# Two-block transformer forward on one core: a new order of TensorE's steps and of its PSUM banks in the forgetting attention

## The chip, the cores and the metric

One NeuronCore of a Trainium2 chip runs one program. The metric is device time in microseconds from launch to end. The kernel before takes 2098.56 us, the median of 3 runs that lie between 2098.52 and 2100.52 us.

## The reference, cut to what matters

The reference applies two transformer blocks to x, 512 tokens of width 1024. The change touches only the mixer of the first block (and the place where it meets the second step of that block, the memory attention):

```python
z = h @ w_in                        # h = rms_norm(x); columns: a, g, q, k, v, f
u = a * sigmoid(g)
u = causal_depthwise_conv(u, conv_w, conv_b)         # 31 taps, 512 channels
u = silu(layer_norm(u, conv_ln_g, conv_ln_b))
log_f = log_sigmoid(f_logit + b_forget)
# forgetting attention, 8 heads of 64, blocks of 128 queries, causal
logits = q k^T * scale + cum[q] - cum[k]             # cum = cumsum(log_f)
att = softmax(mask(logits)) @ v
y = concat([u, att]) @ w_out
...
mem_n = rms_norm(mem)                                # 256 memory tokens
k_mem = mem_n @ w_mk                                 # used one stage later
```

## The kernel before, in words

Tokens lie along the free dimension (512 columns), features along the partitions. Each engine has one hand-written program in `build`, and semaphores tie them together; every instruction starts in the order of its own program. All products are float32 split in a high and a low part, so that one product is three matmuls (`mm3`, three calls of line 159). Weights come in chunks of 1 MB (`CHUNKS`): SP loads chunk n into one of two staging tiles, ACT copies the high part (`weights(n)`), POOL subtracts it to get the low part (`weights(n)` of POOL, tile WL), and TensorE waits for both before a chunk's first product. ACT's copy of chunk n waits until TensorE is done with chunk n-2.

PSUM has eight banks. `open_bank` takes the next in turn and waits until its last tenant is freed; two banks are reserved (`co`) as sums of the convolution for as long as VectorE works on it.

The stage of the forgetting attention runs so on TensorE: eight steps of gemm `ag`, then the values (`v`, four banks, 96 matmuls over chunks 6 and 7), a small column sum `ms`, then the query and key tiles. A tile `qk n` (24 matmuls of 512 columns) holds queries (n even) or keys (n odd) of two heads. Tiles 0, 1 and 2 come first, then the logits of head 0, `fox_s(0)` (four mask products and eight products), then tile 3, and then a loop over the eight heads h:

- `fox_t(h)`: ten transposes of the normalised weights PP into three banks `ft`.
- `fox_s(h+1)`: the next head's logits, in three banks `fs`.
- `qk_tile(h+4)`, for h up to 3: a whole tile.
- `fox_pv(h)`: 12 matmuls with V, in bank `fo`.
- for h = 0 the spread of the memory norm `mr`; for h = 4 the total `cmu` of the convolution's channels; for h = 5 the memory keys of chunk 12 (`mem_k(0, 0, 1)`); for h = 6 one column sum `cq2`, one tile of chunk 13 and the spread `crs`; for h = 7 the other tile of chunk 13.

Then gemm `wo` (w_out) starts with chunk 14 and walks k = 0 to 7; k = 0 to 3 is the convolution's output (HH, HL), k = 4 to 7 are the heads in pairs (CATH, CATL).

What the other engines do for a head: VectorE takes the four row maxima (`fox_max`, TENSOR_REDUCE), ACT the exponentials, VectorE the reciprocals (`fox_rcp`), ACT the four norms into PP (`fox_norm`). After the transposes ACT writes PTH (`fox_turned`) and VectorE PTL, which also frees the `ft` banks. After `fox_pv` ACT writes CATH (`fox_high`) and VectorE CATL (`fox_low`), which frees `fo`. For a tile `qk n` VectorE scales it in place (`qk_out`), ACT copies the high parts (`qk_high`), VectorE subtracts the low ones, which frees the bank, and POOL makes twins of the high parts for the other half of the partitions (`twins`).

Beside that runs the depthwise convolution with its 31 taps for each of four groups of channels: VectorE does most (`convolve(n, 3)` issues the next n taps of a list), ACT and POOL share 25 taps of group 1: ACT makes a product into one of four tiles TP (`products`), POOL adds it (`taps`); product w waits for tap w-4. POOL sums the groups (`cacc`), TensorE's `cmu` turns that into a mean, VectorE subtracts it (`xc`), ACT squares (`csq`), POOL adds the squares (`c2acc`), the column sum `cq2` and a root give the norm, and after `crs` VectorE scales the groups (`xn_`), ACT applies the silu and VectorE writes HL. The memory tokens are scaled on VectorE (`scaled_memory`), split by ACT (`memory_high`) and POOL.

## Time and profile before

| what | value |
|---|---|
| median of 3 runs | 2098.56 us |
| the profiled execution's own time | 2100.5 us |
| its span, first to last instruction | 2098.7 us |
| PE busy | 2011.9 us, 96% |
| DVE / ACT / POOL busy | 1272.0 / 861.7 / 983.0 us |
| mean granted clock of TensorE | 0.990 |

Matmuls are pipelined: a matmul's duration in a row is longer than the distance to the next one, and the distance is what a stream costs. An idle time stands in square brackets behind a row with what ended it. A row may merge several instructions (x10) and then hide waits between them.

### The profile page before, as it was taken

The numbers are of one execution on the slowest core, as the hardware profiler recorded it, in microseconds if no ns is written. First come the engines' busy times: TensorE is split into PE (matmuls) and PEld (weight loads), VectorE is DVE, ScalarE is ACT, GpSimd is POOL, SyncE is SP. The second block draws the span as 40 slices with busy tenths as digits, with TensorE's granted clock in tenths as the row PEclk, the third lists the DMA queues.
The fourth block names the chain that finished last, engine by engine and source line by source line (L and its number), as shares of the span: only waits on it lengthen the run. The fifth ranks groups of instructions, "written<-read, shape, count | busy, mean of one in ns | idle before, by whom it ended". The sixth has DMA issues, their size and how long they took to land.

```text
span 2098.7 us, 23678 instructions
## 1 busy us (share of the span) xinstructions
PE 2011.9 (96%) x9667; PEld 1672.6 (80%) x9667; DVE 1272.0 (61%) x1568; ACT 861.7 (41%) x1254; POOL 983.0 (47%) x476
## 2 busy tenths in 40 slices
PE   6999989999999999999999999999998999999997
PEld 4777778778888887787888888878887888888886
DVE  7677845462245435663677775545679657778644
ACT  5746775631122234774443333232322244333322
POOL 5579454454444433123444444444667654444443
PEclk9999999999999999999999999999999999999999
DMA  6432123112222230121222222215222312222221
GB/s 206 154 123 81 41 81 106 65 71 101 101 99 86 97 113 27 43 71 47 71 86 98 101 101 100 84 63 185 101 71 101 121 61 101 100 101 92 89 101 40
DMA packets 35041, 193.00 MB, mean 92 GB/s; under 512 B 4400, under 2 KB 4992, under 8 KB 15413
## 3 DMA queue, kind: packets, MB, share of 16 engines
q1 hardware_dynamic: 34932, 191.49, 26.1%
q8 instruction: 76, 1.25, 0.3%
q14 instruction: 33, 0.26, 0.0%
HBM read 177.77 MB, written 13.64 MB: 91 GB/s over the span
## 4 chain that ended last, share of the span: by engine, by line
PE 77%; DVE 11%; ACT 6%; POOL 4%; issue 2%; DMA 0%; SPq 0%; ACTq 0%; DVEq 0%; POOLq 0%
PE ps L159 73%; PE ps L158 3%; DVE TMP L182 2%; POOL WL L182 1%; POOL CO L182 1%; DVE X L182 1%; DVE X L194 1%; DVE YL L182 1%; PE ps L167 1%; DVE ps L194 1%; POOL YF L182 1%; DVE ps L182 1%; ACT WH L175 1%; ACT PP L176 0%; DVE VG L182 0%
## 5 line engine op out<-in xcount | busy, mean ns | idle before, releaser
L182 POOL TENSOR_TENSOR WL<-W,WH 128x2048 fp32r<-128x2048 f32 (+3 forms) x165 | 650.5, 3948 | 860.5 <-ACT WH L175 857.0
L159 PE MATMUL ps<-HH,WL 128*128 128x512 f32 (+1 forms) x1408 | 545.6, 388 | 15.4 <-DVE HL L194 7.9
L159 PE MATMUL ps<-HH,WH 128*128 128x512 f32 (+1 forms) x1408 | 538.8, 383 | 0.0
L159 PE MATMUL ps<-HL,WH 128*128 128x512 f32 (+1 forms) x1408 | 538.8, 383 | 0.0
L175 ACT ACTIVATE WH<-W 128x2048 fp32r<-128x2048 f32 (+2 forms) x145 | 269.4, 1858 | 316.8 <-PE ps L159 316.8
L159 PEld LDWEIGHTS ps<-HH,WL 128*128 128x128 f32 x1408 | 265.3, 188 | 74.9 <-DVE HL L194 9.9
L159 PEld LDWEIGHTS ps<-HH,WH 128*128 128x128 f32 x1408 | 265.2, 188 | 51.9
L159 PEld LDWEIGHTS ps<-HL,WH 128*128 128x128 f32 x1408 | 265.6, 189 | 50.7 <-issue 0.2
L182 DVE TENSOR_TENSOR MRL<-MID,MRH 128x512 fp32r<-128x512 f32 x76 | 177.4, 2365 | 162.3 <-ACT MRH L175 162.3
L159 PE MATMUL ps<-MRH,WL 128*128 128x512 f32 x608 | 238.2, 392 | 3.3 <-ACT PAD L175 2.2
L159 PE MATMUL ps<-MRH,WH 128*128 128x512 f32 x608 | 236.7, 389 | 0.0
L159 PE MATMUL ps<-MRL,WH 128*128 128x512 f32 x608 | 236.6, 389 | 0.0
L182 DVE TENSOR_TENSOR MID<-TMP,TMP 128x512 f32<-128x512 f32 x44 | 175.8, 3996 | 30.7 <-ACT TMP L176 30.7
L175 ACT ACTIVATE PAD<-ps 128x512 f32<-128x512 f32 x88 | 52.6, 600 | 273.0 <-PE ps L159 273.0
L194 DVE SCALAR_TENSOR_TENSOR TMP<-PAD,PAR,TMP 128x512 f32<-128x512 f32 x176 | 140.7, 800 | 6.2
L159 PEld LDWEIGHTS ps<-MRH,WL 128*128 128x128 f32 x608 | 114.2, 188 | 28.3 <-ACT PAD L175 3.0
L159 PEld LDWEIGHTS ps<-MRL,WH 128*128 128x128 f32 x608 | 114.2, 188 | 23.9 <-issue 0.5
L159 PEld LDWEIGHTS ps<-MRH,WH 128*128 128x128 f32 x608 | 114.1, 188 | 23.9
L182 DVE TENSOR_TENSOR TMP<-ps,TMP 128x512 f32<-128x512 f32 x36 | 24.8, 690 | 111.4 <-PE ps L159 104.8
L182 POOL TENSOR_TENSOR TMP<-TMP,TMP 128x512 f32<-128x512 f32 x47 | 62.7, 1334 | 63.2 <-ACT TMP L176 61.5
L194 DVE SCALAR_TENSOR_TENSOR X<-X,ps 128x512 f32<-128x512 f32 (+1 forms) x36 | 22.5, 627 | 110.4 <-PE ps L159 110.3
L188 DVE TENSOR_SCALAR TMP<-PAD,PAR 128x512 f32<-128x512 f32 x88 | 42.2, 480 | 72.4 <-ACT PAD L175 72.4
(370 smaller groups left out, 3284.3 us busy)
## 6 DMA issues: line engine op xcount, KB each, us to landing
W<-in_up SPq DMA_DIRECT2D x44, 1024.0 KB, 4.8
W<-in_down SPq DMA_DIRECT2D x22, 1024.0 KB, 4.8
W<-in_w_up SPq DMA_DIRECT2D x16, 1024.0 KB, 4.8
W<-in_w_down SPq DMA_DIRECT2D x16, 1024.0 KB, 4.8
W<-in_hy_in SPq DMA_DIRECT2D x12, 1024.0 KB, 4.8
kd<-STG SPq DMA_DIRECT2D x36, 256.0 KB, 2.0
KB<-kd SPq DMA_DIRECT2D x8, 1024.0 KB, 5.8
W<-in_win_ag SPq DMA_DIRECT2D x4, 1024.0 KB, 4.8
```

What stands on the lines that cost most here:

```text
L158: return self.eng.matmul(out, lhs, rhs, start=start, stop=stop, skip_group_check=True)
L159: return self.eng.matmul(out, lhs, rhs, start=start, stop=stop)
L167: return QUIET if self.eng is None else self.eng.transpose(out, src, ident)
L175: return self.eng.activation(out, src, fn, scale=scale)
L182: return QUIET if self.eng is None else self.eng.tensor_tensor(out, a, b, op)
L188: return self.eng.tensor_scalar(out, a, s1, None, o1)
L194: return self.eng.scalar_tensor_tensor(out=out, in0=a, scalar=s, in1=b, op0=o1, op1=o2)
```

## The change

TensorE: tiles `qk` 0 and 1 move ahead of the values, and w_in's first query and key chunk moves ahead of the values' chunks (it becomes chunk 6, the values' 7 and 8). After the values come `ms`, the logits of head 0 and tile 2. In the loop, tiles 3 to 7 come one a head for h = 0 to 4, each cut in halves of 12 matmuls before and after the next head's logits; for h = 5 the memory keys of chunk 12 take their place, cut in the same way. The fourth mask product of a head moves behind the products of the first three blocks. `cmu` moves from h = 4 to h = 2. Banks are no longer taken in turn but named (`on(i)`): `here` are the three banks of this head's logits, `there` the others, and they change places at each head's end. For h = 6 the column sum runs over the four tiles of squares instead of one sum of them, and `crs` moves to h = 7. The first chunk of w_out is written out as `out_first`, in the order k = 4, 5, 6, 0, 1, 2, 3, 7, in banks `there[0:2]`.

VectorE: the taps are spread anew (2, 6 and 20 before the values' low parts, 3 after each of three of them, 6 in head 0, 3 and all that are left in head 1); `xc`, the memory's scaling and the last scaling move to other heads. ACT: `weights`, `products`, `qk_high` and the memory's parts stand elsewhere; the squares of the convolution go to POOL. POOL: two more taps ahead of `weights(8)`, and the memory's low parts ahead of the last twins. SP's program is unchanged, but the order of its loads follows `CHUNKS`.

```diff
@@ -53,8 +53,8 @@
 CHUNKS = [
-    ("dft_cs", 0, 2048), ("dft_kx", 0, 256), *[("win_ag", i, 2048) for i in range(4)], *[("win_v", i, 2048) for i in range(2)],
-    *[("win_qk", i, 2048) for i in range(4)], *[("w_mk", i, 2048) for i in range(2)],
+    ("dft_cs", 0, 2048), ("dft_kx", 0, 256), *[("win_ag", i, 2048) for i in range(4)], ("win_qk", 0, 2048),
+    *[("win_v", i, 2048) for i in range(2)], *[("win_qk", i, 2048) for i in range(1, 4)], *[("w_mk", i, 2048) for i in range(2)],
     *[("w_out", i, 2048) for i in range(4)],
     *[("w_mv", i, 2048) for i in range(2)],
     *[("w_mq", i, 2048) for i in range(2)], *[("w_mo", i, 2048) for i in range(2)],
...
@@ -745,6 +745,21 @@
     gemm("ag", CH["win_ag"][2:4], 8, 2, feat, lambda k: ("hn", 0, k), base=4, head=False)
+    def on(i):
+        turn[0] = i
+    def qk_steps(n, first, last):
+        wh, wl = chunk(CH["win_qk"][n // 2])
+        ps = bank("qk", n) if first else open_bank("qk", n)
+        for k in range(first, last + 1):
+            col = (2 * k + n % 2) * 128
+            ins = pe.mm3(ps[:], wh[:, col:col + 128], wl[:, col:col + 128], *feat(k), k == 0, k == 7)
+        if last == 7:
+            ins.then_inc(*up(acc, ("qk", n), *[("w_used", CH["win_qk"][n // 2])] * (n % 2)))
+    qk_steps(0, 0, 7)
+    qk_steps(1, 0, 7)
...
+    g0, g1 = bank_of["qk", 0], bank_of["qk", 1]
+    v0, v1, v2, v3 = [bank_of["v", b] for b in range(4)]
+    c0, c1 = bank_of["co", 0], bank_of["co", 1]
+    on(v0)
     column_sum([(("ms",), MSQ[:, 0, :], ("msum", 1), None, ("ms",))], nb=2)
-    def qk_tile(n):
-        if n >= 8:
-            return
-        wh, wl = chunk(CH["win_qk"][n // 2])
-        ps = open_bank("qk", n)
-        for k in range(8):
-            col = (2 * k + n % 2) * 128
-            ins = pe.mm3(ps[:], wh[:, col:col + 128], wl[:, col:col + 128], *feat(k), k == 0, k == 7)
-        ins.then_inc(*up(acc, ("qk", n), *[("w_used", CH["win_qk"][n // 2])] * (n % 2)))
-        for i in (0, 2, 3):
-            open_bank("fs", h, max(i, 1))
-        for i in range(4):
+        def mask(i):
+            if i != 1:
+                on(places[max(i - 1, 0)])
+                open_bank("fs", h, max(i, 1))
             nk = 128 * (i + 1)
             pe.mm(logits(h, i)[:, nk - 128:nk], IDR[:], MKR[:], i != 1, False, True)
+        for i in range(3):
+            mask(i)
...
         for i in range(4):
+            if i == 3:
+                mask(3)
...
-    qk_tile(0)
-    qk_tile(1)
-    qk_tile(2)
-    fox_s(0)
-    qk_tile(3)
+    def cat_tile(k):
+        return feat(k) if k < 4 else (CATH[k - 4][:], CATL[k - 4][:])
+    def out_first(places):
+        n = CH["w_out"][0]
+        wh, wl = chunk(n)
+        for m, i in enumerate(places):
+            on(i)
+            open_bank("wo", m, hold=True)
+        for k in (4, 5, 6, 0, 1, 2, 3, 7):
+            pe.wait_ge(*at("cat", k))
+            for m in range(2):
+                col = (2 * k + m) * 128
+                rh, rl = cat_tile(k)
+                ins = pe.mm3(bank("wo", m)[:], wh[:, col:col + 128], wl[:, col:col + 128], rh, rl, k == 4,
+                             k == 7)
+                if k == 7:
+                    ins.then_inc(*up(acc, ("wo", m), *[("w_used", n)] * m))
+                    close("wo", m)
+    fox_s(0, (g0, g1, v1))
+    on(v2)
+    qk_steps(2, 0, 7)
+    here, there = [g0, g1, v1], [v0, v2, v3]
     for h in range(8):
-        fox_t(h)
+        fox_t(h, here)
+        if h < 5:
+            on(there[2])
+            qk_steps(h + 3, 0, 3)
+        if h == 5:
+            mem_k(0, (0, 1), 0, 3, (c0, c1))
         if h < 7:
-            fox_s(h + 1)
+            fox_s(h + 1, (there[0], there[1], here[0]))
+        if h < 5:
+            qk_steps(h + 3, 4, 7)
+        if h == 5:
+            mem_k(0, (0, 1), 4, 7)
+        if h == 6:
+            on(there[2])
+            column_sum([(("cq2",), CO2[:, j, :], ("csq", j), None, ("cq2",) if j == 3 else None)
+                        for j in range(4)])
+            mem_k(1, (0,), 0, 7, (here[2],))
         if h == 7:
-            mem_k(1, 1)
-        qk_tile(h + 4)
-        fox_pv(h)
+            mem_k(1, (1,), 0, 7, (c0,))
+            on(c1)
+            spread("crs", slot=20)
+        fox_pv(h, here[1])
         if h == 0:
+            on(here[2])
             spread("mr", slot=28, nb=2)
-        if h == 4:
-            total("cmu", ap=DG[:], need=("cacc", 3))
+        if h == 2:
             close("co", 0)
             close("co", 1)
-        if h == 5:
-            mem_k(0, 0, 1)
-        if h == 6:
-            column_sum([(("cq2",), CO2[:, 0, :], ("c2acc", 3), None, ("cq2",))])
-            mem_k(1, 0)
-            spread("crs", slot=20)
-    def cat_tile(k):
-        return feat(k) if k < 4 else (CATH[k - 4][:], CATL[k - 4][:])
+            on(c0)
+            total("cmu", ap=DG[:], need=("cacc", 3))
+        here, there = [there[0], there[1], here[0]], [there[2], here[1], here[2]]
...
@@ -864,7 +911,8 @@
-    gemm("wo", CH["w_out"], 8, 2, cat_tile, lambda k: ("cat", k))
+    out_first(there[0:2])
+    gemm("wo", CH["w_out"][1:], 8, 2, cat_tile, lambda k: ("cat", k), base=2, head=False)
...
@@ -1472,24 +1520,11 @@
     act.act(MSQ[:], MX0[:], ACT.Square, ROOT_D).then_inc(*out(("msq",)))
-    weights(7)
-    products(5, 8)
-    weights(8)
-    for b in range(4):
-        act.wait_ge(*at("v", b))
-        act.wait_ge(*at("inv", "xs"))
-        act.act(VH[:, b, :], bank("v", b)[:], ACT.Identity, SM[:, 4 + b:5 + b]).then_inc(*out(("vv", b, "hi")))
-        if b == 3:
-            weights(9)
-        products(9 + 2 * b, 10 + 2 * b)
-    root(("ms",), 24, "eps6", 2)
     def qk_high(n):
-        if n >= 8:
...
@@ -1498,6 +1533,22 @@
+    weights(7)
+    products(5, 8)
+    qk_high(0)
+    products(9, 12)
+    qk_high(1)
+    weights(8)
+    products(13, 16)
+    weights(9)
+    for b in range(4):
+        act.wait_ge(*at("v", b))
+        act.wait_ge(*at("inv", "xs"))
+        act.act(VH[:, b, :], bank("v", b)[:], ACT.Identity, SM[:, 4 + b:5 + b]).then_inc(*out(("vv", b, "hi")))
+        if b < 3:
+            products(17 + b, 17 + b)
+    root(("ms",), 24, "eps6", 2)
     def expo(group, dst, nk, scale, slot, *need):
...
@@ -1561,40 +1612,43 @@
         act.wait_ge(*now(act_tile))
         high(HH[:, j, :], CO[:, j, :], ("cat", j))
-    qk_high(0)
-    products(17, 20)
-    qk_high(1)
-    products(21, 24)
-    qk_high(2)
+    weights(10)
     fox_exp(0)
     fox_norm(0)
-    qk_high(3)
+    products(20, 22)
+    qk_high(2)
     for h in range(8):
-        if h > 5:
-            mem_k_high(*((0, 1), (2,))[h - 6])
         fox_turned(h)
+        if h == 0:
+            products(23, 24)
+        if h == 6:
+            mem_k_high(0, 1)
         if h < 7:
             fox_exp(h + 1)
             fox_norm(h + 1)
-        if h == 4:
-            memory_high(0, 3)
-        if h == 7:
+        else:
+            weights(14)
+            mem_k_high(2)
             for j in range(4):
                 silu(j)
-        qk_high(h + 4)
+        if h == 1:
+            weights(11)
+        if h == 3:
+            memory_high(0, 3)
+        if h == 4:
+            memory_high(4, 7)
+        if h == 5:
+            weights(13)
+        if h == 6:
+            root(("cq2",), 16, "eps6", 4, 1.0 / 512)
+        if h < 5:
+            qk_high(h + 3)
         fox_high(h)
         if h == 0:
             act.wait_ge(*at("mr"))
             act.copy(MRS[:], bank("mr")[:, 0:256]).then_inc(*out(("mrs",), ("free", "mr")))
-        if h == 5:
-            memory_high(4, 7)
-            for j in range(4):
-                act.wait_ge(*at("xc", j))
-                act.act(CO2[:, j, :], CO[:, j, :], ACT.Square, 512.0 ** -0.5).then_inc(*out(("csq", j)))
-            weights(13)
-        if h == 6:
-            root(("cq2",), 16, "eps6")
-            weights(14)
+        if h == 2:
+            weights(12)
     mem_k_high(3)
...
@@ -2226,30 +2280,29 @@
     gated(3)
-    for b in range(4):
-        convolve(4, 3)
-    for b in range(4):
-        dve.wait_ge(*at("vv", b, "hi"))
-        dve.stt(VL[:, b, :], bank("v", b)[:], SM[:, 4 + b:5 + b], VH[:, b, :].bitcast(F), ALU.mult,
-                ALU.subtract).then_inc(*out(("vv", b), ("free", "v", b)))
-        convolve(2, 3)
...
                 *[("free", "qk", n)] * e)
-        if n < 2:
-            convolve(4, 3)
+    convolve(2, 3)
+    qk_out(0)
+    convolve(6, 3)
+    qk_out(1)
+    convolve(20, 3)
+    for b in range(4):
+        dve.wait_ge(*at("vv", b, "hi"))
+        dve.stt(VL[:, b, :], bank("v", b)[:], SM[:, 4 + b:5 + b], VH[:, b, :].bitcast(F), ALU.mult,
+                ALU.subtract).then_inc(*out(("vv", b), ("free", "v", b)))
+        convolve((3, 3, 3, 0)[b], 3)
...
@@ -2293,45 +2346,48 @@
-    qk_out(0)
-    qk_out(1)
-    qk_out(2)
+    def centred(first, last):
+        for j in range(first, last + 1):
+            dve.wait_ge(*at("cmu"))
+            dve.stt(CO[:, j, :], bank("cmu")[:], -1.0 / 512, CO[:, j, :], ALU.mult, ALU.add).then_inc(
+                *out(("xc", j), *[("free", "cmu")] * (j == 3)))
     fox_max(0)
     fox_rcp(0)
-    qk_out(3)
+    qk_out(2)
     for h in range(8):
-        if h > 5:
-            mem_k_low(*((0, 1), (2,))[h - 6])
         for j in range(3):
             q = turned(j)
             low(PTL[:, q], bank("ft", h, j)[:, 0:q.stop - q.start], PTH[:, q], ("pt", h, j), ("free", "ft", h, j))
+        if h == 6:
+            mem_k_low(0, 1)
         if h < 7:
             fox_max(h + 1)
-            convolve(3, 3)
-            if h in (4, 5):
-                scaled_memory(4 * h - 16, 4 * h - 15)
+            if h == 1:
+                convolve(3, 3)
+            if h in (3, 4):
+                scaled_memory(4 * h - 12, 4 * h - 9)
             fox_rcp(h + 1)
-            if h in (4, 5):
-                scaled_memory(4 * h - 14, 4 * h - 13)
-        convolve(4, 3)
+        if h == 0:
+            convolve(6, 3)
+        if h == 1:
+            convolve(200, 3)
+        if h in (3, 4):
+            centred(2 * h - 6, 2 * h - 5)
         if h == 7:
-            for j in range(4):
-                low(HL[:, j, :], CO[:, j, :], HH[:, j, :], ("cat", j))
-        qk_out(h + 4)
-        fox_low(h)
-        if h == 4:
-            convolve(200, 3)
-            dve.wait_ge(*at("cmu"))
-            for j in range(4):
-                dve.stt(CO[:, j, :], bank("cmu")[:], -1.0 / 512, CO[:, j, :], ALU.mult, ALU.add).then_inc(
-                    *out(("xc", j), *[("free", "cmu")] * (j == 3)))
-        if h == 6:
-            inverse(("cq2",), 16, [("col", "crs")])
             weights(CH["w_out"][0])
             dve.wait_ge(*at("crs"))
             for j in range(4):
                 dve.tt(CO[:, j, :], CO[:, j, :], bank("crs")[:], ALU.mult).then_inc(
                     *out(("xn_", j), *[("free", "crs")] * (j == 3)))
+            mem_k_low(2)
+            for j in range(4):
+                low(HL[:, j, :], CO[:, j, :], HH[:, j, :], ("cat", j))
+        if h < 5:
+            qk_out(h + 3)
+        fox_low(h)
+        if h == 6:
+            inverse(("cq2",), 16, [("col", "crs")])
     mem_k_low(3)
     def post(s, Y, g, g2):
...
@@ -3037,12 +3093,13 @@
     weights(7)
-    taps(5, 8)
+    taps(5, 10)
     weights(8)
-    taps(9, 14)
+    taps(11, 16)
     weights(9)
-    taps(15, 24)
+    taps(17, 19)
...
@@ -3050,20 +3107,28 @@
     next_rows(6)
-    twins(5)
-    next_rows(7)
-    twins(6)
-    weights(12)
-    twins(7)
     for j in range(1, 4):
         pool.wait_ge(*at("tap", j, 30))
         if j > 1:
             pool.wait_ge(*at("cacc", j - 1))
         pool.tt(DG[:], CO[:, 0, :] if j == 1 else DG[:], CO[:, j, :], ALU.add).then_inc(*out(("cacc", j)))
-    for k in range(8):
-        pool.wait_ge(*at("hm", k, "hi"))
-        pool.low(HML[:, k, :], tmp("mn", k)[:, 0:256], HMH[k]).then_inc(*out(("hm", k), ("tf", "mn", k)))
-    add_up(CO2[:, 0, :], lambda j: CO2[:, j, :], 3, ("csq",), ("c2acc",))
+    next_rows(7)
+    twins(5)
+    weights(12)
+    def memory_low(first, last):
+        for k in range(first, last + 1):
+            pool.wait_ge(*at("hm", k, "hi"))
+            pool.low(HML[:, k, :], tmp("mn", k)[:, 0:256], HMH[k]).then_inc(*out(("hm", k), ("tf", "mn", k)))
+    memory_low(0, 3)
+    twins(6)
+    memory_low(4, 7)
+    twins(7)
+    for j in range(4):
+        pool.wait_ge(*at("xc", j))
+        pool.wait_ge(*at("qk", 7))
+        pool.tt(CO2[:, j, :], CO[:, j, :], CO[:, j, :], ALU.mult).then_inc(*out(("csq", j)))
     weights(13)
```

## Rows read from the trace of the kernel before

**Rows 1.** The page: the span, and busy time of each engine.

```profile
span 2098.7 us, 23678 instructions
PE 2011.9 (96%) x9667; PEld 1672.6 (80%) x9667; DVE 1272.0 (61%) x1568; ACT 861.7 (41%) x1254; POOL 983.0 (47%) x476
```

**Rows 2.** Stretches: length, busy time of PE, PEld, DVE, ACT, POOL, PEclk, DMA share, GB/s.

```profile
152.00:306.00 154.00, 139.64 (x732) 118.46 (x731) 107.21 (x191) 110.66 (x216) 98.05 (x76) 0.96 0.19 69
205.00:211.00 6.00, 5.86 (x18) 5.16 (x19) 5.14 (x11) 2.90 (x10) 3.97 (x7) 0.50 0.43 167
265.00:270.00 5.00, 4.70 (x22) 4.60 (x23) 4.41 (x12) 3.11 (x11) 0.00 (x0) 0.66 0.00 0
1408.00:1410.00 2.00, 2.00 (x9) 1.66 (x10) 2.00 (x4) 2.00 (x4) 0.60 (x1) 1.00 0.00 0
```

**Rows 3.** Who PE waited for, 150 to 300 us: total, times, longest.

```profile
PE ps L158 <- DVE PTL L182: 3.8, 2, 2.8
...
PE ps L158 <- DVE CATL L182: 3.2, 4, 1.3
```

**Rows 4.** Timeline of PE: start, duration, line, operation, idle before.

```profile
152.13 0.47 PE L159 MATMUL ps<-WH,HL 128*128 128x512 f32 x1
...
173.98 0.58 PE L158 MATMUL ps<-ONE,MSQ 128*128 128x96 f32 x4
...
201.79 3.18 PE L167 MATMUL ps<-IDT,PP 128*128 128x128 f32 x10 [3.32 <-DVE ps L194]
...
249.53 0.39 PE L158 MATMUL ps<-PTH,VL 128*128 128x512 f32 x1
...
251.39 1.28 PE L167 MATMUL ps<-IDT,PP 128*128 128x128 f32 x10
253.37 0.63 PE L158 MATMUL ps<-MKR,IDR 128*128 128x128 f32 x4 [0.70 <-DVE CATL L182]
...
255.16 0.40 PE L158 MATMUL ps<-PTH,VL 128*128 128x512 f32 x1
...
280.82 1.08 PE L158 MATMUL ps<-ONE,CO 128*128 128x96 f32 x8
...
1407.91 0.50 PE L159 MATMUL ps<-HH,WL 128*128 128x512 f32 x1 [2.44 <-POOL HL L182]
```

**Rows 5.** Timeline of POOL: taps of group 1, and the low part of a chunk.

```profile
162.34 5.41 POOL L182 TENSOR_TENSOR CO<-CO,TP 128x512 f32<-128x512 f32 x4
167.70 4.63 POOL L182 TENSOR_TENSOR WL<-W,WH 128x2048 fp32r<-128x2048 f32 x1
```

**Rows 6.** Timeline of ACT.

```profile
218.08 0.37 ACT L175 ACTIVATE MRS<-ps 128x256 f32<-128x256 f32 x1
...
286.48 1.90 ACT L175 ACTIVATE WH<-W 128x2048 fp32r<-128x2048 f32 x1
...
288.54 1.36 ACT L175 ACTIVATE PTH<-ps 128x512 fp32r<-128x512 f32 x3
289.92 1.28 ACT L176 ACT_TABLE_LOAD   x1
291.21 0.82 ACT L176 ACTIVATE CO<-CO,PAR 128x512 f32<-128x512 f32 x1
...
296.83 0.59 ACT L175 ACTIVATE CATH<-ps 64x512 fp32r<-64x512 f32 x1
```

**Rows 7.** Timeline of DVE.

```profile
222.17 2.06 DVE L194 SCALAR_TENSOR_TENSOR ps<-U,PAR,ps 128x512 f32<-128x512 f32 x3
...
226.97 0.69 DVE L194 SCALAR_TENSOR_TENSOR ps<-ps,TMP 128x512 f32<-128x512 f32 x1
228.32 1.41 DVE L182 TENSOR_TENSOR QKB<-ps,QKA 64x512 fp32r<-64x512 f32 x2 [0.66 <-ACT QKA L175]
...
254.79 1.67 DVE L206 TENSOR_REDUCE SM<-ps 128x1 f32<-128x128 f32 x4
...
257.61 0.18 DVE L200 RECIPROCAL SM<-SM 128x4 f32<-128x4 f32 x1 [0.24 <-ACT PP L173]
```

33 lines of the change are left out of this document (17 added, 16 removed).

## The prediction

> **What bounds the kernel now.** I read the page first: PE is busy for 2011.9 of 2098.7 us [rows 1], so only what TensorE does, and where it waits, sets the end. Second, the stretches: in the 154.0 us of this stage PE is busy for 139.6, so it stands still for 14.4 us, and its granted clock is 0.96 there [rows 2]. Third, who PE waited for: two low parts of VectorE hold 7.0 us of it, PTL with one wait of 2.8, and CATL, which frees the bank of the head before, with four [rows 3]. Fourth, the timeline, for what the busy time hides. Ten transposes take 3.18 us at 201.79 and 1.28 at 251.39 [rows 4]: 1.9 us are waits inside a merged row. And the clock: after the wait of 3.32 us it is at 0.50 (1.2 GHz in place of 2.4) from 205 to 211, which loses 3.0 us, and after the wait of 2.8 us it averages 0.66 for 5 us, which loses 1.7 [rows 2, 3, 4]. Together the stage holds 14.4 + 1.9 + 3.0 + 1.7 = 21.0 us in which PE does not work at its speed. This is the most that the change could take away; outside the stage it touches nothing.
>
> **What PE does a head.** 96 matmuls of 512 columns take 173.98 - 152.13 = 21.85 us, 0.228 each: a tile of 24 takes 5.4, its half 2.7 [rows 4]. The product with V takes 251.39 - 249.53 = 1.9, the logits 255.16 - 253.37 = 1.8, the transposes some 1.0 (1.28 less the tail that overlaps the next) [rows 4]. From the end of the logits to the reciprocals pass 257.61 - 255.16 = 2.45 us, to the end of the maxima 1.3 [rows 4, 7].
>
> **What the change wins.** The first transposes no longer follow a wait for tile 3, the halves put 2.7 us between the transposes and the next logits, so CATL (3.2 us of waits) is covered, and a tile covers head 5's chain, which was bare. I count all 21.0 us as gone, and then count what comes in their place, edit by edit.
>
> **Work, +3.0.** One column sum becomes four. One is 8 matmuls in 1.08 us [rows 4]; three more are 3.2, a little less as rows overlap: 3.0. ACT's squares and POOL's sums become four products on POOL, 5.41 / 4 = 1.35 each by its adds [rows 5], in head 5; between 0.6 and 1.4 each they end ahead of the column sum of head 6. Nothing on the path.
>
> **A: the second chunk of the values, +3.7.** PE starts tile 0 at 152.13 as it started the values, ends tile 1 10.9 us later at 163.0 and the values' first half at 173.9; there it needs chunk 8. ACT copies chunk 8 only behind products(9, 12) and qk_high(1). POOL's taps begin at 162.34 as before, 1.35 each [rows 5]. Product 12 waits for tap 8, at 162.34 + 4 x 1.35 = 167.7, and ends some 0.7 later (0.82 for an activation of the same size [rows 6]): 168.4. The two high copies and two twins behind it take 2.5 (0.59 for one of 64x512 [rows 6]), the copy 1.90: 172.8. POOL has then ended its six taps (170.4), takes 4.63 for the low part [rows 5] and is done at 177.4. PE waits from 173.9 to 177.6. Before, the eighth chunk's low part stood two taps earlier on POOL and had no tile's copies ahead of it on ACT. SP's loads keep their order by chunk and 1 MB each; each is free to go more than 10 us ahead of its copy, so none of them counts.
>
> **The first transposes, +0.8.** The values end at 188.4, logits and tile 2 at 196.1. On ACT stand behind the values: a copy 0.6, the root with its table 1.5, chunk 10 1.9, the table of the exponential 1.3, four exponentials 2.2 (of the 2.45 above); reciprocals and norms follow, the first at 196.4, the last ending at 198.3. So the transposes end 1.6 later than PE could. Bounds 0 and 1.6; I take the middle.
>
> **B: tile 4, +3.3.** By the head's times PE ends the transposes of head 0 at 198.7, half of tile 3 at 201.4, logits at 203.2, the other half at 205.9, V at 207.8, mr at 208.3 and the transposes of head 1 at 209.3. Tile 4 goes to the bank there[2], which is here[2] of head 0: the place of mr. It is free when ACT has copied MRS, behind qk_high(3) and CATH. VectorE has reciprocals at 205.7 and then six taps of 0.66 (2.06 for three, overlapping [rows 7]) before it scales tile 3: 209.7, scaled 210.4; ACT's two copies 1.2, CATH 0.6, MRS 0.37 [rows 6]: 212.5. PE waits 3.3.
>
> **C: head 3's logits, +5.5.** From 212.6 PE does half a tile, logits (217.2), half a tile, V, transposes, half a tile: 225.5. The mask of head 3 goes to tile 4's bank. VectorE ends the maxima at 218.5, has 3 and then 11 taps left in head 1 (14 x 0.66 = 9.2: 227.7), and scaling and low parts of tile 4 take 2.8 (226.97 to 229.73 [rows 7]): 230.5. The second mask wants the bank of head 1's V, whose low part CATL comes 0.7 later. 5.0 and 0.5. Before, the same taps stood seven to a head, each group behind other cover.
>
> **Small waits, +1.2.** In head 5 the halves are 1.5 us each, so the norms end behind them; in head 6 CATH of head 5 stands behind chunk 13's copy (1.90 [rows 6]), and a bank waits for it; head 6's logits want the twins of tile 7, behind four low parts on POOL. My bounds are 0 and 2.5; I take the middle.
>
> **D: the first product of w_out, +6.0.** This is what I find most telling. After head 7's swap there[1] is here[1] of head 7, the bank of its V. out_first opens both banks before its first matmul, so PE waits until VectorE has written CATL of head 7. That is the last step of all: from the end of the transposes, T, ACT does PTH 1.36, chunk 14 1.90, one memory key 0.3, then table, four silus and CATH, 289.92 to 297.42 = 7.5 [rows 6], then VectorE 0.7: T + 11.8. PE needs 2.9 for the memory tile, 1.0 for the spread and 1.9 for V: T + 5.8. Before, the eight steps began with this chain still running, since nothing but k = 7 needs it; the order 4, 5, 6, 0 to 3, 7 would still allow it, the bank doesn't.
>
> **The clock, +6.8.** A, B, C and D are each as long as the 3.32 and 2.8 us that let the clock fall, or longer. The rows bound what one such wait costs behind it: nothing after 2.44 us at 1407.91 (clock 1.00), 1.7 us at 265, 3.0 us at 205 [rows 2, 4]. I take 1.7 for each of four, the middle one.
>
> **Sum.** 3.0 + 3.7 + 0.8 + 3.3 + 5.5 + 1.2 + 6.0 + 6.8 = 30.3, less 21.0: +9.3 us. It is made against the profiled execution, whose span is 2098.7 and whose own time is 2100.5, 1.9 above the median; I add it to the median: 2098.6 + 9.3 = **2107.9 us**. About 0.2%, 4.2 us, is what a measurement of this kernel can tell from no change.
>
> **Where a page speaks against the change.** A table load on ACT takes 1.28 us here, and the next instruction starts at once, 289.92 to 291.21 [rows 6]. The Trainium skill, page "ScalarE: Activation LUTs", section "What ACT_TABLE_LOAD costs", adds a drain of some 1.38 us to each switch, 2.66 in all. The chain of the first transposes holds two switches and that of D one; by the page those waits would grow by 3 x 1.38, an estimate of 4.1 us. The trace disagrees with it.
>
> **The rivals.**
> 1. VectorE keeps ahead of the heads (not slower). 37 of the taps are done by the end of the values. If tile 3 is scaled before PE ends tile 3's second half and V, which means by 207.8 where I have 210.4, B and C vanish with their two falls of the clock: 9.3 - 3.3 - 5.5 - 3.4 = -2.9, 2095.7 us. It decides at the six taps in head 0. For it: 46.8 us of the stage VectorE is idle now [rows 2]. Against it: those taps are written ahead of the scaling. Chance 0.12, of which 0.08 for under 2094.4, as small terms fall away too.
> 2. The clock holds as after 2.44 us [rows 2, 4]: 9.3 - 6.8 = +2.5, 2101.1 us. Chance 0.08: all four waits are longer than the two that let it fall.
> 3. All at the upper bounds: clock 3.0 each, 1.6 and 2.5 for the small ones: 25.6 + 12.0 - 21.0 = +16.6, 2115.2 us. Chance 0.09.
> 4. A switch of tables costs the chains of the first transposes and of D a second load's time, three times 1.28 [rows 6]: 9.3 + 3.8 = +13.1, 2111.7 us. Chance 0.03, since no load of the trace does it. The drain of the Trainium skill's page named above would be such a mechanism.
> My forecast keeps 0.68, of which 0.04 lies under 2102.8 us. Slower: 0.64 + 0.09 + 0.03 = 0.76; the same: 0.04 + 0.08 + 0.04 = 0.16; faster 0.08. The range, 2099 to 2115, leaves out rival 1 and the edge of rival 3.
>
> **What would show it.** In the profile after: WL of a chunk named as what ended a PE wait near 174 to 178; a wait of 3 to 4 us ended by ACT MRS near 210; one near 226 to 231 ended by VectorE's QKA or QKB low part; a wait of about 6 us right ahead of w_out's first matmul, ended by CATL; PEclk 0.5 behind several of them; CATL no longer behind four waits of the middle heads. Wrong if the stage is shorter than 154 us, if VectorE's taps end before head 1's logits, or if w_out starts with no wait.

## The result and the profile after

The changed kernel takes 2106.5 us (median of seven runs, 2104.8 to 2107.2) where the kernel before takes 2099.9: a ratio of 1.0033, 95% interval 1.0023 to 1.0043. A second measurement, beside three of the experiments below and on their chip, gave 2106.9 (six runs, 2104.0 to 2113.1) against 2098.7, 1.0043 (1.0031 to 1.0055). So the change costs 7 to 8 us. The forecast was 2107.9, slower, with a range of 2099 to 2115.

The top of the page, to set beside [rows 1]:

```profile
span 2103.0 us, 23723 instructions
PE 2009.2 (96%) x9691; PEld 1672.3 (80%) x9691; DVE 1272.3 (61%) x1568; ACT 860.4 (41%) x1250; POOL 983.5 (47%) x477
```

PE is busy for 2.7 us less than before in a span 4.3 us longer. What the stage lost stands in two views. First, who PE waited for from 150 to 320 us (total, times, longest), beside [rows 3]:

```profile
PE ps L159 <- DVE CATL L182: 6.1, 1, 6.1
PE ps L158 <- DVE QKA L182: 4.2, 1, 4.2
PE ps L159 <- POOL WL L182: 3.7, 1, 3.7
PE ps L159 <- ACT MRS L175: 3.3, 1, 3.3
PE ps L158 <- DVE CATL L182: 1.6, 2, 1.3
```

The rows of before are gone: no PTL, and CATL only twice between heads. Four waits that before did not have take their place, and each is the longest of its row. Second, the stretches behind three of those waits (A, C and D below), beside [rows 2]; the column ahead of the last two is the clock that was granted:

```profile
152.00:306.00 154.00, 132.87 (x716) 114.38 (x715) 106.91 (x191) 106.57 (x210) 95.43 (x76) 0.94 0.19 68
...
176.00:178.00 2.00, 1.79 (x4) 1.50 (x5) 2.00 (x4) 0.67 (x1) 1.92 (x3) 0.50 0.45 90
...
234.00:236.00 2.00, 2.00 (x8) 1.85 (x8) 1.96 (x6) 0.47 (x3) 1.84 (x3) 0.50 0.88 369
...
300.00:302.00 2.00, 1.99 (x5) 1.62 (x6) 0.32 (x1) 1.99 (x3) 0.00 (x0) 0.50 0.00 0
302.00:304.00 2.00, 2.00 (x7) 1.52 (x6) 0.00 (x0) 0.75 (x1) 1.17 (x1) 0.50 0.00 0
304.00:306.00 2.00, 2.00 (x7) 1.60 (x6) 0.00 (x0) 0.00 (x0) 2.00 (x1) 0.66 0.00 0
306.00:308.00 2.00, 2.00 (x10) 1.65 (x9) 0.00 (x0) 0.00 (x0) 1.41 (x1) 1.00 0.00 0
```

In the same 154 us PE is busy for 132.9 us where it was for 139.6 [rows 2], at a clock of 0.94 for 0.96. Behind each wait stand some 3.4 us at 1.2 GHz, behind the last twice as much.

PE's own rows date the four waits A to D and show the four column sums:

```profile
176.21 0.77 PE L159 MATMUL ps<-WH,HL 128*128 128x512 f32 x1 [3.68 <-POOL WL L182]
...
213.57 0.77 PE L159 MATMUL ps<-HH,WL 128*128 128x512 f32 x1 [3.35 <-ACT MRS L175]
...
232.64 0.44 PE L158 MATMUL ps<-MKR,IDR 128*128 128x128 f32 x2 [4.20 <-DVE QKA L182]
...
278.71 3.71 PE L158 MATMUL ps<-ONE,CO 128*128 128x96 f32 x32
282.20 0.36 PE L159 MATMUL ps<-HM,WL 128*128 128x256 f32 x1
...
300.01 0.77 PE L159 MATMUL ps<-CATH,WL 128*128 128x512 f32 x1 [6.07 <-DVE CATL L182]
```

To compare traces I use one measure: the **stage** runs from the start of the first tile and the values (10.9 us ahead of the values' first matmul in the changed kernel, that matmul itself before) to the start of the matmul behind w_out's first 48, so that a wait between the two counts to the stage; the **rest** is all behind it. Before: 152.13 to 305.98, 153.8 us. After: 150.6 to 313.5, 162.9 us, or 9.1 us more.

### The profile page after: what moved, and what is told of

Same layout as the page of the kernel before. It is cut to its first block, busy times and chain, and to the rows that moved or that the text cites. A ratio compares the mean times of both kernels' runs of the same rounds, so it can differ in the third digit from the quotient of the medians.

```text
span 2103.0 us, 23723 instructions
## 1 busy us (share of the span) xinstructions
PE 2009.2 (96%) x9691; PEld 1672.3 (80%) x9691; DVE 1272.3 (61%) x1568; ACT 860.4 (41%) x1250; POOL 983.5 (47%) x477
## 3 DMA queue, kind: packets, MB, share of 16 engines
q8 instruction: 76, 1.25, 0.3%
## 4 chain that ended last, share of the span: by engine, by line
PE 78%; DVE 11%; ACT 6%; POOL 4%; issue 2%; DMA 0%; SPq 0%; ACTq 0%; DVEq 0%; POOLq 0%
PE ps L159 73%; PE ps L158 3%; DVE TMP L182 2%; POOL WL L182 1%; DVE X L182 1%; DVE X L194 1%; DVE YL L182 1%; DVE ps L194 1%; PE ps L167 1%; POOL CO L182 1%; POOL YF L182 1%; DVE ps L182 1%; ACT WH L175 1%; DVE VG L182 0%; ACT PM L173 0%
## 5 line engine op out<-in xcount | busy, mean ns | idle before, releaser
L159 PE MATMUL ps<-MRL,WH 128*128 128x512 f32 x608 | 236.6, 389 | 0.0
```

Source lines behind the costliest of these rows:

```text
L159: return self.eng.matmul(out, lhs, rhs, start=start, stop=stop)
```

## The experiments

All are edits of the changed kernel, except where said. The rows of the tables are worked out from PE's timelines and from stretches. The first table gives for each trace the start of its stage, the stage, the rest, how often the clock fell in the rest ahead of the last matmul (each time some 3.4 us at 1.2 GHz, from stretches of 2 us), and the median of the runs beside it.

Start, stage and rest add up to the span of the one execution that was traced, which can lie at either end of its runs: 2104.8 us was the lowest of seven in the first trace of the changed kernel. The kernel before has 2098.5 to 2098.7 us beside these medians, and 2099.9 beside the first of the changed kernel. Where A was not edited, its wait is 3.6 to 3.7 us in five traces and 2.2 to 2.3 in five others (see the end), so stages are compared with the trace of the changed kernel that has the same A: the second for "free banks", "work in the wait", "free banks and chunk 15" and "whole tiles", the first for the others.

| trace | starts | stage | rest | falls | median |
|---|---|---|---|---|---|
| before | 152.1 | 153.8 | 1792.8 | 3 | 2098.6 |
| changed | 150.6 | 162.9 | 1789.5 | 1 | 2106.5 |
| changed, again | 151.8 | 161.0 | 1793.5 | 4 | 2106.9 |
| free banks | 155.1 | 154.5 | 1795.6 | 4 | 2106.5 |
| free banks, again | 152.3 | 157.1 | 1795.8 | 4 | 2106.5 |
| chunk 8 first | 152.0 | 159.0 | 1789.5 | 1 | 2102.3 |
| MRS first | 152.2 | 159.7 | 1789.4 | 1 | 2107.6 |
| taps moved | 152.2 | 160.4 | 1792.6 | 3 | 2106.1 |
| work in the wait | 152.1 | 158.2 | 1792.7 | 3 | 2107.2 |
| free banks and chunk 15 | 153.6 | 153.8 | 1793.9 | 4 | 2103.1 |
| one sum | 152.4 | 160.8 | 1791.2 | 2 | 2108.5 |
| whole tiles | 155.0 | 168.8 | 1792.6 | 3 | 2117.3 |
| all four | 150.6 | 145.8 | 1789.4 | 1 | 2092.0 |
| all five | 152.0 | 143.8 | 1790.8 | 1 | 2088.6 |

**D: free banks for w_out's first products.**

```diff
-            out_first(there[0:2])
+            out_first((there[2], here[2]))
```

> Edit: w_out's first two products take the banks of head 7's first tile half and its last (free long before) in place of the pair in which head 7's V lies; nothing else. My theory: the wait of 6.07 us ended by CATL of head 7, right ahead of w_out, is one for the bank alone, and the half clock in the 6 us behind it (a loss of 2.7 us by the stretches) comes from it. Both go: at most a wait of 0.4 us for the low part of chunk 14 is left, and the time falls by 8.3 us against the changed kernel, to about 2098.2 us. Rival: PE would wait for the data of head 7 all the same, since the eight steps reach k = 7 too early; then the wait only moves behind the seventh step and the gain is under 3 us. A third: the clock falls later anyway, gain 6.

Measured: 2106.5 us, ratio to before 1.0034 (1.0022 to 1.0046). The whole time did not move, where 8.3 us less were expected; the stage did, by 6.5 us and by 5.8 in a second trace. PE's rows at the place where the 6.07 stood, and 48 matmuls later:

```profile
296.49 0.47 PE L159 MATMUL ps<-CATH,WL 128*128 128x512 f32 x1 [0.54 <-issue]
...
309.58 0.47 PE L159 MATMUL ps<-HH,WL 128*128 128x512 f32 x1 [1.96 <-POOL WL L182]
```

```profile
312.00:314.00 2.00, 2.00 (x6) 1.62 (x5) 0.00 (x0) 0.00 (x0) 2.00 (x1) 0.50 0.83 344
```

The wait of 6.07 is 0.54, so it was for a bank and not for data: k = 7 comes 9.6 us later and finds CATL written. The low part of chunk 15 is next to be late, 1.96 us, and the clock falls behind that wait (0.50 from 312 to 314). That the rest took the gain back is followed up in the last experiment.

**D and what came behind it.** On ACT `weights(15)` goes behind `mem_k_high(2)` of head 7, ahead of the silus, with the free banks as above.

> Edit: the free banks for w_out's first two products, as before, and on ACT the high copy of chunk 15 goes ahead of the table load and the four silus; with the banks alone w_out's second chunk then waited 1.96 us for the low part that POOL makes of that copy. My theory: both waits go, and at most 0.6 us ahead of the first product is left; w_out's first chunk takes 10.9 us, at full clock. Stage: 153.5 to 154.5 us, that is 8.9 less than the changed kernel's; whole time 2097 to 2099 if the falls of the clock elsewhere are as many as in the changed kernel. Rival: the copy delays the silus by 1.9 us and the fifth to eighth step of w_out wait for them: then 2 us are lost again between the third step and the last.

Measured: 2103.1 us, 1.0022 (1.0014 to 1.0031). The stage is 153.8 us, 7.2 under the changed kernel's second trace, which shares with it the short wait at A. The second wait is gone; 0.75 us for the low part of the first silu took its place, ended by DVE HL, a small piece of the rival. The stage came as expected, the whole time is 4 us over its 2097 to 2099: the rest has four falls here.

**The clock at D alone.** Work of no use in the wait:

```diff
+            pe.wait_ge(*at("free", "ft", 7, 0))
+            keep_busy(24, CH["w_out"][0], "ft", 7, 0)
             out_first(there[0:2])
```

> Edit: 24 matmuls of no use run in the changed kernel's wait ahead of w_out's first product, into a bank of head 7 that is free; some 5.5 us of work in a wait of 6.07. Nothing else. My theory: the wait keeps its end, but the granted clock stays at 1.00 in the 8 us behind it, which loses 3.4 us in the changed kernel; w_out's first chunk takes 10.9 to 11.2 us in place of 13.5 to 14.4, the time falls by 3.4, to about 2103. Rival: the clock falls behind these 8 us for what went before (two transposes, a spread, products) and the dummies change nothing: same time.

PE's rows and the stretches behind them:

```profile
293.00 5.66 PE L158 MATMUL ps<-WH,IDR 128*128 128x512 f32 x24
299.24 0.47 PE L159 MATMUL ps<-CATH,WL 128*128 128x512 f32 x1 [0.58 <-DVE CATL L182]
```

```profile
302.00:304.00 2.00, 2.00 (x11) 1.65 (x10) 0.00 (x0) 0.00 (x0) 1.93 (x1) 1.00 0.00 0
```

The clock holds, and w_out's first 48 matmuls take 11.0 us in place of 13.5 (13.7 in the second trace). So the clock costs 2.5 to 2.7 us at D, not 3.4, since its first 0.7 fall into the wait. The stage is 2.8 us shorter than in the second trace of the changed kernel; the median (2107.2) did not come down to the expected 2103.

**A: chunk 8 ahead of the products.**

```diff
             qk_high(0)
-            products(9, 12)
-            qk_high(1)
             weights(8)
-            products(13, 16)
+            qk_high(1)
+            products(9, 16)
...
-            taps(5, 10)
+            taps(5, 6)
             weights(8)
-            taps(11, 16)
+            taps(7, 14)
```

> Edit: ACT copies chunk 8 (the values' second half) right behind the first high copies, ahead of four products, and POOL makes its low part behind two taps in place of six; the other taps and products move behind, none is dropped. My theory: the wait of 3.7 us in the middle of the values is for this chunk's copies alone, and the 1.4 us at half clock behind it come with it. Time: 5.1 us less than the changed kernel, about 2101.4 us. Rival: the products that are moved behind delay ACT's and POOL's later work (the first norm, the twins of tile 2, chunk 10), and the first transposes wait longer: then the gain is 2 us or none, and a wait ended by PTL or PTH near 197 us is over 2 us.

Measured: 2102.3 us, 1.0025 (1.0014 to 1.0036); the stage is 3.9 us shorter. The values run through in 21.8 us. 1.11 us (ended by VectorE's VL of the values) and 0.45 are new ahead of tile 2 and of head 1's logits, 0.4 less stands at the first transposes: 5.1 less 1.2.

```profile
188.08 0.47 PE L159 MATMUL ps<-HH,WL 128*128 128x512 f32 x1 [1.11 <-DVE VL L194]
```

**B: MRS ahead of the high copies.** On ACT the copy of `mr` goes ahead of `qk_high(h + 3)`.

> Edit: on ACT the copy of the memory's column sums (MRS), which frees the bank for tile 4, goes ahead of the high copies of tile 3 and of head 0's output; nothing else. My theory: the bank of tile 4 is free at 210.6 in place of 213.5 us, PE's wait of 3.35 us ahead of tile 4 goes and with it the clock's fall (1.6 us), but the logits of head 1 then meet the low parts of tile 3 on VectorE: a wait of 0.5 to 1.5 us. Net: 3.5 us less than the changed kernel, about 2103.0. Simple sum of wait and clock: 5.0 less. Rival: VectorE's scaling of tile 3 is what is late, and the order on ACT only names it: then the wait comes back whole at head 1's logits, at 0 to 1 us gain.

Measured: 2107.6 us, 1.0038 (1.0025 to 1.0051). The wait of 3.35 us is gone and 0.49 + 0.27 + 0.29 us stand at head 1's logits and the next transposes; the stage is 3.2 us shorter. The rival, a wait that comes back whole, is out.

```profile
215.12 0.44 PE L158 MATMUL ps<-MKR,IDR 128*128 128x128 f32 x2 [0.49 <-DVE QKB L182]
```

The five runs lie at 2101.5 and 2103.0 (mean granted clock 0.992 and 0.991) and three times at 2107.6 to 2108.5 (0.987). The trace is of the one at 2103.0; where the others lost their clock is not shown. The expected 2103.0 was met by two runs, not by the median.

**C: VectorE's taps.** Five taps go between `fox_max(0)` and `fox_rcp(0)`, three into the scaling of tile 2, and `convolve(6, 3)` in head 0 becomes `convolve(4, 3)`.

> Edit: nine of VectorE's convolution taps change place: five of them go between the maxima and the reciprocals of the first head, three into the scaling of tile 2, so that one is left behind head 0's scaling of tile 3 in place of three and five in head 1 in place of eleven; the number of taps is the same. My theory: the taps ahead of tile 4's low parts are what makes head 3's logits wait 4.5 us (with 1.7 us of half clock), and those ahead of the scaling of tile 3 make 1.35 of the 3.35 us at tile 4. Time: about 7 us less than the changed kernel, 2099.5; bounds 5.3 and 8.6 by whether the clock also holds at tile 4. Rival: the taps only move the wait to the first head, whose reciprocals come 3.4 us later behind the five taps: then the transposes of head 0 wait over 3 us near 197 and the gain is 3 us or less.

Measured: 2106.1 us, 1.0035 (1.0023 to 1.0047), where 2099.5 were expected; stage 2.6 us shorter. Who PE waited for:

```profile
PE ps L159 <- POOL TMP L182: 2.7, 1, 2.7
...
PE ps L158 <- DVE QKA L182: 0.3, 1, 0.3
```

QKA falls from 4.2 to 0.3 and MRS from 3.3 to 2.1, as forecast. But PE now reaches `cmu` of head 2 ahead of POOL's three sums, which stand behind chunk 11's low part: 2.7 us and a fall of the clock. Neither I nor my rival had this wait.

**One column sum again.** POOL adds the squares up (`c2acc`), PE sums one tile of them.

> Edit: in the changed kernel the four column sums of the memory's norm become one again: POOL adds the four squares up (three more sums of 1.35 us) and PE sums one. My theory: on PE the work falls by 2.6 us (3.7 to 1.1), but POOL makes the low part of chunk 13 4 us later (its end 284.4 in place of 280.4, less what POOL stood idle ahead of it, so 280.9), and the memory tile that follows waits for it: a wait of 1 to 1.5 us, ended by POOL WL, takes the place of half of the gain. Stage: 1.3 us less than the changed kernel's. Rival: the four sums are a cost of their own, as my prediction counted them: 2.6 us less. A second rival: POOL's three adds come too late for the column sum itself; then the stage is as long as before or longer.

```profile
280.64 1.03 PE L158 MATMUL ps<-ONE,CO 128*128 128x96 f32 x8
282.75 0.35 PE L159 MATMUL ps<-HM,WL 128*128 128x256 f32 x1 [1.08 <-issue]
```

```profile
270.06 8.08 POOL L182 TENSOR_TENSOR CO<-CO 128x512 f32<-128x512 f32 x7
278.09 4.55 POOL L182 TENSOR_TENSOR WL<-W,WH 128x2048 fp32r<-128x2048 f32 x1
```

PE does 2.5 us less work and waits 1.08 in its place. The row names no other engine, but PE goes on 0.1 us behind the end of POOL's low part of chunk 13 at 282.6, so from the logits to the memory tile 2.1 us pass in place of 3.5. Nearly half of the extra work was cover for that copy; before, the same copy was waited for 1.65 us there. The median, 2108.5 (1.0047), did not follow.

**Whole tiles in place of halves.**

```diff
-                    qk_steps(h + 3, 0, 3)
+                    qk_steps(h + 3, 0, 7)
...
-                if h < 5:
-                    qk_steps(h + 3, 4, 7)
```

> Edit: the tiles of 24 products for heads 3 to 7 stand whole between the transposes and the next logits, not in two halves around the logits; the order of the other work and the banks stay. My theory: the halves win by covering both ends of a head, the bank of the head before (CATL) ahead of the logits and the exponentials behind them. Whole, 2.45 us from the logits to the reciprocals and 0.5 for the first norm have only the 1.9 us of V over them: the transposes of heads 1 to 5 wait 1.1 us or more each and again 0.5 inside them, ended by ACT PP; the stage is 5 to 8 us longer than the changed kernel's, in which the wait of 4.2 us at head 3 may lose up to 2. Whole time 2109 to 2115. Rival: the gain lies in the order of the whole (first tiles, head 5's cover) and a whole tile would do as well: within 2 us of the changed kernel.

```profile
PE ps L167 <- ACT PP L176: 7.1, 14, 1.7
```

Measured: 2117.3 us, 1.0091 (1.0076 to 1.0106), slower than the expected 2109 to 2115; the stage is 7.8 us longer than in the second trace of the changed kernel (5.9 than in the first). PE waits 14 times for a normalised block, 7.1 us (three times, 1.2 us, before the edit). The halves do win what they seem to be made for.

**The four moves together.** A to D, chunk 15 as above, and on POOL the three sums go ahead of `weights(11)`.

> Edit: the four moves together (chunk 8 ahead of the products; MRS ahead of the high copies; nine taps of VectorE moved; free banks for w_out), with two more: chunk 15's copy ahead of the silus, and on POOL the three sums for the column mean ahead of chunk 11's low part, since with the taps alone PE waited 2.73 us for these sums. My theory: the four waits and the clock's falls behind them are independent costs; by the stages measured one by one (-3.9, -3.2, -2.6 and -2.7 for the sums, -8.9) the stage comes to 141.6 us, and the whole to about 2085, between 2082 and 2089; faster than both kernels. Rival: with PE ahead of them by 15 us, the three other engines set the pace, and the waits come back at other places: the stage is over 148 us and the whole over 2092.

```profile
PE ps L167 <- ACT PP L176: 3.3, 5, 2.4
...
PE ps L159 <- DVE VL L194: 1.1, 1, 1.1
```

Measured: 2092.0 us, 0.9963 (0.9951 to 0.9975), faster than both kernels, but over the expected 2082 to 2089. The stage is 145.8 us, not 141.6: the waits A to D are gone together, but their costs do not simply add up. The five taps I had moved ahead of the first reciprocals now lie bare, 2.40 us and a fall of the clock, and 1.12 and 0.73 us stand at the values and in w_out. This is part of what the rival said (waits that come back at other places), though the stage stays under its 148 us.

**All five.** The taps are placed again.

```diff
-                convolve((3, 3, 3, 0)[b], 3)
+                convolve((3, 0, 3, 2)[b], 3)
...
             fox_max(0)
+            convolve(2, 3)
             fox_rcp(0)
```

> Edit: the four moves together as before, with the places of VectorE's taps chosen again: two ahead of the first reciprocals in place of five, seven inside the scaling of tile 2, and none between the second and the third low part of the values; chunk 15's copy behind the first silu. The combined version waited 2.40 us (and 1.7 of clock) at the first transposes, 1.12 for a bank of the values and 0.73 in w_out. My theory: the reciprocals come 2 us earlier, the wait of 2.40 falls under 1.3, that of 1.12 and of 0.73 go, and the clock holds near 196: the stage goes from 145.8 to 141.5 us, the whole to 2087.5, between 2085 and 2091. Rival: ACT sets the first transposes, by its two tables and its copy of chunk 10, not the taps: then the wait stays at 2 us or over, and the stage at 144 or more.

```profile
PE ps L167 <- ACT PP L176: 2.3, 6, 1.1
...
PE ps L159 <- DVE HL L182: 1.3, 1, 1.3
```

```profile
152.00:296.00 144.00, 136.36 (x755) 116.97 (x756) 111.28 (x191) 108.42 (x212) 98.96 (x77) 1.00 0.23 81
```

Measured: 2088.6 us, 0.9956 (0.9944 to 0.9969): 10 us under the kernel before. The clock is at 1.00 through the stage; first transposes wait 1.14 us, 143.8 us in all. That is 2 us over my figure: with chunk 15's copy behind the first silu PE waits 1.25 us for a silu's low part, where it had waited 0.73, and 0.89 us for a low part ahead of head 1's logits are new. The interval overlaps that of the four moves, so the 3 us between their medians are not shown to be a gain; 2.1 us of the stage are.

**What the time outside the stage does.** Two kernels were run a second time, unchanged.

> The changed kernel itself, unchanged, beside the next ones, so that they are compared on one chip and with a second trace of it. In the first traces the falls of the clock outside this stage were not the same from one profile to the next, each 1.7 us or twice that. My theory: the waits of this stage come back to 0.1 us and at the same places (3.7, 3.3, 4.2, 6.1), while the falls behind the short waits at 50, 102, 130, 1412, 1604 and 1654 us come and go; stage 162.9 us give or take 1.7, whole time 2106 give or take 2. Rival: the falls outside the stage belong to the kernel; then the trace has none of them, as the first one of it.

> The kernel with free banks for w_out alone, unchanged, a second time. Its first trace had a stage shorter by 6.5 to 8.4 us, yet its whole time was that of the changed kernel: the trace began the stage 3.3 to 4.5 us later, in work ahead of the edit, and showed falls of the clock at 50, 102, 130, 1412, 1604 and 1654 us. Theory one, chance: falls outside the stage come and go from one execution to the next; the second trace shows the same waits in the stage (6.07 gone, 1.96 in its place), other falls outside, and the median comes down to 2102, between 2100 and 2104. Theory two, the kernel: moved by 6 us, the later waits of 2.0 to 2.5 us fall where they let the clock go, in every execution; then the falls at 1412, 1604 and 1654 are there again and the median is 2106 to 2107 once more.

The second trace of the changed kernel repeats the waits at B, C and D within 0.02 us, has 2.34 at A in place of 3.68, with no fall behind it, a fall of twice the length at C (229.8 to 236.6 us, in part inside the wait), and three falls behind 1412 us that the first had not. Its stretches, and those of the first trace at the same step:

```profile
128.00:130.00 2.00, 2.00 (x6) 1.07 (x5) 1.89 (x4) 0.75 (x2) 2.00 (x4) 0.50 0.00 0
...
176.00:178.00 2.00, 1.95 (x9) 1.65 (x10) 2.00 (x4) 0.73 (x1) 1.92 (x2) 1.00 0.56 90
...
1606.00:1608.00 2.00, 2.00 (x6) 1.52 (x6) 1.59 (x3) 0.00 (x0) 1.92 (x3) 0.50 1.03 422
```

```profile
1606.00:1608.00 2.00, 2.00 (x13) 1.66 (x12) 1.69 (x4) 0.00 (x0) 1.92 (x3) 1.00 1.04 424
```

PE waits 2.31 and 2.32 us for the same step in both, but only one is followed by 1.2 GHz. The free banks gave 2106.5 us again, with the same three falls at 1412, 1604 and 1654:

```profile
1414.00:1416.00 2.00, 2.00 (x6) 1.63 (x5) 2.00 (x4) 2.00 (x4) 1.29 (x1) 0.50 0.03 8
...
1656.00:1658.00 2.00, 2.00 (x6) 1.62 (x5) 1.97 (x4) 0.72 (x2) 2.00 (x3) 0.50 1.04 438
```

The signs of theory two came. They do not prove it: both traces are of executions at the upper end (2107.0 us), four of the eleven runs of this kernel lie at 2104.2 to 2104.7 and have no trace, and "changed, again" has the same three falls without the edit.

What each fall costs can be read, for between the waits that all traces share the distances take only two values (the end of a wait, to the end of the next):

| from | to | no fall ahead | with a fall ahead |
|---|---|---|---|
| end of the stage | wait near 437 | 124.1 to 124.2 | 125.9 (at 311, behind the wait at 309) |
| wait near 437 | wait near 1412 | 977.7 to 977.8 | 977.6 to 977.9 |
| wait near 1412 | wait near 1604 | 188.9 | 190.0 to 190.2 |
| wait near 1604 | wait near 1654 | 50.2 | 51.7 to 51.8 |
| wait near 1654 | last instruction | 448.5 to 448.6 | 450.1 to 450.2 |

So the rest is 1789.5 us plus 1.8, 0, 1.2, 1.6 and 1.6 for the falls at the five places, within 0.4 us in all fourteen traces; the fall behind 437 us is free (11 traces have it, 3 not). For the free banks this says more than the count of falls: of the 6 us that their rest is longer than that of the first trace of the changed kernel, 1.8 belong to the edit, behind the wait of 1.96 us for chunk 15 that it laid bare, and 4.4 are the three later falls. Beside the second trace, which has these three too, their rest is only 2.1 and 2.3 us longer. What decides whether a fall follows was not found. The edit itself brings the later steps only 3.2 to 4.1 us forward at the end of the stage (309.6 and 309.4 us in place of 313.5 and 312.8), and 1.3 to 2.3 near 1412.

## Why the prediction was right

| term | forecast | measured in the changed kernel's trace |
|---|---|---|
| four column sums | 3.0 | 2.4: 3.5 us from 278.71 to 282.20, less the 1.08 of [rows 4] |
| A, chunk 8 | 3.7 | 3.68 |
| first transposes | 0.8 | 1.21 in three waits |
| B, bank of mr | 3.3 | 3.35 |
| C, head 3's logits | 5.5 | 4.20 + 0.29 |
| small waits | 1.2 | 0.96 + 1.27 |
| D, w_out | 6.0 | 6.07 |
| clock | 6.8 | 7.2: 1.4, 1.4, 1.8 and 2.6 |
| sum | 30.3 | 30.6 |
| losses of before, gone | 21.0 | 21.5, by difference |
| stage | +9.3 | +9.1 |

What the three other engines did ahead of the four waits, from the timelines of ACT, POOL and VectorE in the changed kernel (start, length, what ended the idle time before it):

```profile
169.53 1.92 ACT L175 ACTIVATE WH<-W 128x2048 fp32r<-128x2048 f32 x1
171.53 4.54 POOL L182 TENSOR_TENSOR WL<-W,WH 128x2048 fp32r<-128x2048 f32 x1 [2.60 <-ACT WH L175]
...
211.34 1.21 ACT L175 ACTIVATE QKA<-ps 64x512 fp32r<-64x512 f32 x2 [2.61 <-DVE ps L194]
213.06 0.36 ACT L175 ACTIVATE MRS<-ps 128x256 f32<-128x256 f32 x1
...
222.61 6.00 DVE L194 SCALAR_TENSOR_TENSOR ps<-U,PAR,ps 128x512 f32<-128x512 f32 x9
228.51 1.40 DVE L194 SCALAR_TENSOR_TENSOR CO<-U,PAR,ps 128x512 f32<-128x512 f32 x2
231.18 1.41 DVE L182 TENSOR_TENSOR QKA<-ps,QKA 64x512 fp32r<-64x512 f32 x2 [0.66 <-ACT QKA L175]
...
291.13 1.28 ACT L176 ACT_TABLE_LOAD   x1
292.82 0.82 ACT L176 ACTIVATE CO<-CO,PAR 128x512 f32<-128x512 f32 x1 [0.41 <-DVE CO L182]
...
298.44 0.59 ACT L175 ACTIVATE CATH<-ps 64x512 fp32r<-64x512 f32 x1
299.17 0.69 DVE L182 TENSOR_TENSOR CATL<-ps,CATH 64x512 fp32r<-64x512 f32 x1
```

Point by point:

- **What goes.** All losses of before were counted as gone, and the stage agrees to 0.5 us. One of them had in the main a wrong name: the 1.9 us "inside" the ten transposes at 201.79 [rows 4] I called waits. In stretches of 2 us the clock of before is already at 0.50 there, so the transposes ran at half speed, 0.21 us apart in place of 0.11, which makes 2.3 of the 3.18; only some 0.8 us are left for waits, for ACT's norms. From 200 to 212 the clock took 5.1 us, the first quarter of a us inside the wait, where I had 1.9 + 3.0:

```profile
202.00:204.00 2.00, 1.83 (x7) 1.15 (x7) 0.32 (x1) 1.98 (x5) 1.94 (x3) 0.50 0.00 0
```

- **A** came out as reasoned. ACT began the copy of chunk 8 at 169.53, behind its products and the high copies and twins of tile 1, and ended it at 171.4, where I had 172.8. POOL's low part followed at once and ended at 176.1, and PE went on at 176.2. That the figure is met to 0.02 us is luck: in the second trace of the same kernel the wait is 2.34.
- **B** likewise: VectorE scaled tile 3 behind six taps, and behind ACT's copies MRS ended at 213.4.
- **C** is one of two terms that were mis-sized by 1 us, 5.5 for 4.5. The taps and low parts of VectorE stand there as written, and moving them took the wait away. But from the end of B to the wait PE took 14.9 us (213.57 to 228.44) where I had 12.9; 1.4 of these 2.0 are the clock's fall behind B, which I had counted as a cost of its own and not as time in which VectorE gets ahead. VectorE's chain was 1.2 longer: 5.0 - 2.0 + 1.2 = 4.2.
- **Small waits** are the other, 1.2 for 2.2. Both stand where the prediction looked for them, the twins of tile 7 at 268.2 (0.96) and the bank ahead of head 7's logits at 277.1 (1.27), but near the upper bound of 2.5 and not in the middle. That C and this term miss by the same 1 us in opposite ways is luck; without it the sum would be 1 us off.
- **D** was right to 0.1 us, and the free banks show its cause: the bank, not the data.
- **The clock** was forecast at 1.7 for each of four waits. It fell behind all four, three times for 1.7 us and at D for 3.4; on the path lie 1.4, 1.4, 1.8 and 2.6. That B, C and D were followed by a fall holds for the second trace too; A, 2.34 us there, was not. Rival 2, that it holds, is out for waits of 3.3 us and more. Its odds were argued from "all four waits are longer than the two that let it fall", which B, 3.3 for 3.32, is not. Rival 3, with 3.0 us for each fall, is out as well: the dearest, at D, cost 2.5 to 2.7.
- **Rival 1**, VectorE ahead of the heads, is out by the waits at B and C. It had one thing right: with the taps in other places the wait at C is 0.27 us.
- **Rival 4**, the drain at a switch of tables, is out: the load at 291.13 ends at 292.41 and the next instruction waits 0.41 us for VectorE's CO, as its row says. The Trainium skill, page "ScalarE: Activation LUTs", section "What ACT_TABLE_LOAD costs", would have 1.38 us of drain there; the trace disagrees, as before.
- **Work, +3.0**, was counted as a cost of its own, and with one sum only 1.4 of the 2.5 came back. The prediction didn't ask what is late next if that work goes; it is chunk 13's low part.
- **The whole.** I carried the stage's +9.3 to the whole, +9.3 on the median. The stage gave 9.1 or 7.2 in two traces and the whole 6.7 and 8.2. The difference between the two traces, 3.3 us in their spans, is falls of the clock outside the stage and the shorter wait at A, which the prediction took as unchanged, and it is nearly as large as A. The figure 2107.9 is 1.4 us over the median; a part of this closeness is chance, since the term by term agreement above is with one of two traces.

What stays open: why the rest of one kernel has one fall in one trace and four in another, and so why the free banks alone gained nothing in their median beyond the 1.8 us that their own new wait explains. Longer stretches of the kernel behind 320 us were not changed in any run.

## What to carry to other kernels

A bank is a wait: when banks are named by hand, write beside each the last writer and the last reader of its former content, and give the first product of the next stage a bank that was free long ago. Cutting a tile around a short step covers both of its ends, but what was written between those ends on the other engines (taps, copies, sums) must be moved too, since each wait that goes uncovers the next in line. Judge such an edit by the length of its stage in two traces as well as by the median, because falls of the clock elsewhere hid up to 6 us of gain here (the rest went from 1789.4 to 1795.8 us).
